# A fused five-layer block on one core: in the mixed layer the selection mask is added by TensorE, the convolution taps run on GpSimd, and search rounds and projection tiles are spread anew

## The reference

```python
def short_conv_mixer(a_in, gate_c, gate_b, conv_w):      # 256 channels, 3 taps, causal
    h = gate_c * a_in
    y = depthwise_conv3(h, conv_w)
    return gate_b * y

def dsa_mixer(q, k, v, iq, ik, iw, bias_tab):            # 4 heads of 64
    sc = relu(einsum("bqhd,bsd->bqhs", iq, ik))          # 8 index heads
    score = einsum("bqh,bqhs->bqs", iw, sc) * idx_scale
    score = where(s <= t, score, -inf)
    _, sel = top_k(score, 128)                           # 128 keys per query
    logits = q . k[sel] * 64**-0.5 + bias                # softmax over the selected keys
    ...

def moba_mixer(q, k, v, bias_tab):                       # 4 heads, all causal keys at 512 tokens
    ...

mix = concat([short_conv, pool_mixer, dsa, moba]) @ w_out
```

## Time and profile before

| | |
|---|---|
| three runs | 1729.51, 1732.86, 1734.89 us; median 1732.86 |
| the profiled execution | 1735.27 us, its span 1733.5 us, mean granted TensorE clock 0.991 |
| TensorE busy | 1659.6 us, 96% of the span |
| VectorE, ScalarE, GpSimd busy | 799.1, 768.3, 595.4 us |
| the mixed layer up to its output product | about 1067 to 1262 us from the start of the span |

### The profile page before, as it was taken

One profiled execution on the slowest core, in us unless ns is written; L12 is line 12 of the kernel. 1 busy time (PEld: TensorE's weight loads), 2 busy tenths in 40 slices (PEclk: granted clock), 3 DMA queues, 4 the chain that ended last, 5 costly groups with the idle time before them and its releaser, 6 DMA issues.

```text
span 1733.5 us, 24228 instructions
## 1 busy us (share of the span) xinstructions
PE 1659.6 (96%) x9321; PEld 1349.5 (78%) x9321; DVE 799.1 (46%) x2055; ACT 768.3 (44%) x1565; POOL 595.4 (34%) x286
## 2 busy tenths in 40 slices
PE   7899999999999999999899999998899999999998
PEld 6676779777788787778676778777678888887877
DVE  2777727456353434326677626798433111000052
ACT  4466644456343535433466624425744222212242
POOL 4322233222333323234222133372225444443423
PEclk9999999999999999999999999999999999999999
DMA  6321244232552222144222144522143333333312
GB/s 166 68 43 46 74 144 130 63 77 67 139 164 75 69 67 67 56 146 115 62 44 70 51 153 137 132 73 69 54 134 110 98 97 98 98 97 97 122 61 85
DMA packets 216046, 161.17 MB, mean 93 GB/s; under 512 B 53755, under 2 KB 197147, under 8 KB 215932
## 3 DMA queue, kind: packets, MB, share of 16 engines
q1 hardware_dynamic: 205904, 130.21, 27.0%
q10 hardware_dynamic: 9804, 29.38, 5.4%
q0 software_dynamic: 224, 0.03, 0.1%
HBM read 148.32 MB, written 11.14 MB: 92 GB/s over the span
## 4 chain that ended last, share of the span: by engine, by line
PE 65%; DVE 10%; ACT 5%; issue 2%; POOL 0%; ACTq 0%; DVEq 0%
PE banks L474 18%; PE banks L476 18%; PE banks L475 18%; PE banks L717 3%; PE banks L686 3%; PE banks L732 3%; DVE misc L2548 1%; ACT AB L1434 1%; ACT G L1558 1%; DVE misc L2535 1%; DVE top L2547 1%; DVE AB L2130 1%; ACT w_hi L1304 1%; ACT AB L1460 1%; DVE QKl L1978 1%
## 5 line engine op out<-in xcount | busy, mean ns | idle before, releaser
L2710 POOL TENSOR_TENSOR w_lo<-w_raw,w_hi 128x1024 fp32r<-128x1024 f32 (+3 forms) x253 | 572.8, 2272 | 1110.7 <-ACT w_hi L1304 1102.6
L474 PE MATMUL banks<-XTh,w_hi 128*128 128x512 f32 (+4 forms) x1216 | 452.2, 372 | 14.6 <-DVE w_lo L2431 4.0
L475 PE MATMUL banks<-XTl,w_hi 128*128 128x512 f32 (+4 forms) x1216 | 446.6, 367 | 0.0
L476 PE MATMUL banks<-XTh,w_lo 128*128 128x512 f32 (+4 forms) x1216 | 446.5, 367 | 0.0
L1304 ACT ACTIVATE w_hi<-w_raw 128x1024 fp32r<-128x1024 f32 (+3 forms) x254 | 251.0, 996 | 154.4 <-PE banks L476 110.6
L474 PEld LDWEIGHTS banks<-XTh,w_hi 128*128 128x128 f32 (+1 forms) x1216 | 230.0, 189 | 60.7 <-issue 18.7
L476 PEld LDWEIGHTS banks<-XTh,w_lo 128*128 128x128 f32 (+1 forms) x1216 | 229.9, 189 | 38.1
L475 PEld LDWEIGHTS banks<-XTl,w_hi 128*128 128x128 f32 (+1 forms) x1216 | 230.2, 189 | 36.3
L474 PE MATMUL banks<-w_hi,OTh 128*128 128x512 f32 (+1 forms) x448 | 171.9, 384 | 0.6 <-DVE QKl L1978 0.5
L476 PE MATMUL banks<-w_hi,OTl 128*128 128x512 f32 (+1 forms) x448 | 167.9, 375 | 0.0
L475 PE MATMUL banks<-w_lo,OTh 128*128 128x512 f32 (+1 forms) x448 | 167.7, 374 | 0.0
(11 more groups left out here) (204 smaller groups left out, 2336.6 us busy)
## 6 DMA issues: line engine op xcount, KB each, us to landing
w_raw<-in_w_gate_up_dram SPq DMA_DIRECT2D x44, 512.0 KB, 3.8
w_raw<-in_fox_w_in_dram SPq DMA_DIRECT2D x30, 512.0 KB, 4.1
w_raw<-in_mla_w_in_dram SPq DMA_DIRECT2D x26, 512.0 KB, 4.5
w_raw<-in_w_in_dram SPq DMA_DIRECT2D x24, 512.0 KB, 3.9
w_raw<-in_w_down_dram SPq DMA_DIRECT2D x22, 512.0 KB, 3.5
w_raw<-in_swa_w_in_dram SPq DMA_DIRECT2D x20, 512.0 KB, 3.8
w_raw<-in_mla_w_out_dram SPq DMA_DIRECT2D x16, 512.0 KB, 3.8
x_spill<-AB ACTq DMA_DIRECT2D x16, 512.0 KB, 2.8
```

The lines of the kernel that those rows point to most:

```text
L474: nc.tensor.matmul(o, ah, bh, start=first, stop=False, skip_group_check=True)
L475: nc.tensor.matmul(o, ah, bl, start=False, stop=False, skip_group_check=True)
L476: return nc.tensor.matmul(o, al, bh, start=False, stop=last, skip_group_check=True)
L2710: pool.tensor_tensor(view(w_lo, u, RING), view(w_raw, u, RAW), view(w_hi, u, RING).bitcast(F32), ALU.subtract).then_inc(lo_done, 1)
```

## The change

The change has five parts, all in the mixed layer.

1. **Index block 0 earlier.** TensorE runs `idx_block(0)` before the fourth `iq` tile, which needs only the first two; the fourth tile and the head weights use banks 6 and 7 in place of 2 and 3. ScalarE does the four Relu before it issues five small loads, VectorE the index sums before it evicts the fourth tile.
2. **Convolution taps on GpSimd.** GpSimd gets two new pieces between its `w_lo` instructions: `conv_taps` (per half one multiplication, then twice a multiplication into CONV_A and an addition) and `conv_low` (OTl of the half). VectorE loses its five instructions per half and waits for `conv_s` before it multiplies with CONV_Y.
3. **Search rounds.** In the convolution phase they go from 2, 1, 2, 2, 1 to 3, 3, 3, 3, 3; in the pooling phase they stay 3, 3, 4, 12; the other 11 (18 before) stand in `fill` as 3, 2, 3, 2, 1. As soon as a query tile's rounds are done, its mask is written to SEL_R (three instructions for one).
4. **Mask by TensorE.** For pairs 2 and 3 and t = 1, 2, 3, a product of the identity (rounded once at the start, `ident_r`) with SEL_R[t] adds the mask to the scores in the bank. VectorE's L2126 and L2127 give way to the one L2130 that all other pairs have.
5. **Tiles of the attention phase.** Each q tile goes from `fill(i, 1)` to `fill(i, 0)`, ahead of the turns and scores; the first half of the second values goes from `fill(1, 1)` to `fill(1, 0)`.

```diff
-            place[c.g], place[c.g + 1] = 2, 3
             o = begin()
...
-            tile("iq", n0=P)
...
             for n in range(6):
                 idx_block(n)
+                if n == 0:
+                    tile("iq", n0=P)
                 tile("conv")
...
             def fill(i, pos):                                  # TensorE
-                if pos == 1:
+                if pos == 0:
                     if i < 1:
                         pair_tile("q", i + 3)
+                    elif i == 1:
+                        parts.extend([unit("v"), unit("v")])
+                        value_half(parts, 0)
+                elif pos == 1:
+                    if i < 1:
                         pair_tile("k", i + 3)
                     elif i == 1:
-                        pair_values(2)
+                        value_half(parts, 1)
...
+                    if pr.sel:                                 # TensorE, scores
+                        pe.wait_ge(ident_round, 1)
+                        pe.wait_ge(sel_done, max(pr.s_chunks[ch]))
...
+                        if pr.sel and t:
+                            for x in range(2):
+                                mm = nc.tensor.matmul(bank[2 * (c.sch % 2) + x][:, cols], ident_r[:, :], SEL_R[t],
+                                                      start=False, stop=True, skip_group_check=True)
...
-                            if pr.sel and t:                   # VectorE, maxima
-                                link(nc.vector.tensor_tensor(pr.score(b, x, t), o, pr.bias(t, x), ALU.add))
-                                ins = nc.vector.tensor_tensor_reduce(pr.score(b, x, t), pr.score(b, x, t), SEL[t], 1.0, -3e38,
-                                                                     ALU.add, ALU.max, mx[:, b, 4 * x + t:4 * x + t + 1])
-                                continue
...
             for cc in range(2):                                # VectorE, convolution phase
-                idx_block(3 * cc)
+                if cc:
+                    idx_block(3)
+                    top(3)
                 c.g += 1
-                if cc:
-                    top(2)
                 idx_block(3 * cc + 1)
-                top(2)
+                top(3)
                 o = group()
                 groups_stored(dve, c.g - 1)
                 stored(nc.vector.tensor_tensor(CONV_H[:, 2:514], o[:, :], CONV_A, ALU.mult))
-                groups_stored(dve, c.g)
-                link(nc.vector.tensor_scalar(CONV_Y, CONV_H[:, 0:512], conv_w[:, cc, 0:1], None, ALU.mult))
-                for tap in (1, 2):
-                    link(nc.vector.scalar_tensor_tensor(CONV_Y, CONV_H[:, tap:tap + 512], conv_w[:, cc, tap:tap + 1], CONV_Y,
-                                                        ALU.mult, ALU.add))
                 idx_block(3 * cc + 2)
-                top(1)
+                top(3)
                 o = group()
-                groups_stored(dve, c.g - 1)
+                dve.wait_ge(conv_s, 4 * cc + 4)
+                if cc:
+                    dve.wait_ge(conv_lo, cc)
                 stored(nc.vector.tensor_tensor(otmp[:, :], o[:, :], CONV_Y, ALU.mult))
-                lo(OTl[:, cc, :], otmp[:, :], OTh[:, cc, :])
...
+            def conv_taps(cc):                                 # GpSimd
+
+                groups_stored(pool, mark["conv", cc])
+                pool.tensor_scalar(CONV_Y, CONV_H[:, 0:512], conv_w[:, cc, 0:1], None, ALU.mult)
+                for tap in (1, 2):
+                    pool.tensor_scalar(CONV_A, CONV_H[:, tap:tap + 512], conv_w[:, cc, tap:tap + 1], None, ALU.mult).then_inc(conv_s, 1)
+                    pool.wait_ge(conv_s, 4 * cc + 2 * tap - 1)
+                    pool.tensor_tensor(CONV_Y, CONV_Y, CONV_A, ALU.add).then_inc(conv_s, 1)
+                    pool.wait_ge(conv_s, 4 * cc + 2 * tap)
...
+                if u in (conv0 + 4, conv0 + 7):                # conv0: the first conv unit
+                    conv_taps((u - conv0 - 4) // 3)
+                elif u in (conv0 + 6, conv0 + 9):
+                    conv_low((u - conv0 - 6) // 3)
                 if u == pool0 + 3:
                     window_sums(0)
```

More of the change, by code:

```diff
@@ L581, in pair_values, with value_half @@
                 ready_pv[c.pair + p] = c.g
+            def value_half(parts, half):
+                o = begin()
+                for t in (2 * half, 2 * half + 1):
+                    ts = slice(t * P, (t + 1) * P)
+                    for k in range(KD):
+                        h, l = parts[k // 4]
+                        mm = three(o[:, 256 * (t % 2):256 * (t % 2) + 256], XTh[:, k, ts], XTl[:, k, ts],
+                                   h[:, k % 4, :], l[:, k % 4, :], k == 0, k == KD - 1)
+                end(mm)
             def values(head=0):
@@ L586, in values @@
                 for half in range(2):
[L587 to L594 removed]
+                    value_half(parts, half)
                 released()
@@ L1866, in _, with idx_block @@
             stored(nc.scalar.activation(iw_t[:, :, :], group()[:, 0:3 * IDX_HEADS].rearrange("p (t h) -> p t h", t=3), ACT.Copy))
+            def idx_block(n):
+                keys = CAUSAL_KEYS[1 + n // 2]
+                for h in range(4):
+                    m = 4 * n + h
+                    if h % 2 == 0:
+                        act.wait_ge(idx_s, m // 2 + 1)
+                    if n:
+                        act.wait_ge(idx_f, m - 3)
+                    nc.scalar.activation(RELU[h][:, 0:keys], bank[h][:, 0:keys], ACT.Relu).then_inc(idx_r, 1)
+            idx_block(0)
             act.dma_start(V2, consts["counts"]).then_inc(pool_in, 16)
@@ L2703, in window_sums, with conv_low @@
                 pool.wait_ge(pool_d, cc + 1)
+            conv0 = next(u for u, x in enumerate(units) if x[0] == "conv")
+            def conv_taps(cc):
[6 more added lines that the diff above has]
+                    pool.wait_ge(conv_s, 4 * cc + 2 * tap)
+            def conv_low(cc):
+                pool.wait_ge(g_hi, mark["conv_hi", cc])
+                pool.tensor_tensor(OTl[:, cc, :], otmp[:, :], OTh[:, cc, :].bitcast(F32), ALU.subtract).then_inc(conv_lo, 1)
             pool.wait_ge(pool_cst, 2)
+            pool.wait_ge(cst, N_CST)
             pool.wait_ge(lo_done, 1)
```

101 lines of the change are left out of this document (61 added, 40 removed).

## The result

The changed kernel takes 1741.41 us (median of 7 runs, 1736.68 to 1742.44), the kernel before in the same comparison 1733.29 (7 runs): ratio 1.0046, 95% interval 1.0032 to 1.0060. It is slower, by half a percent, and outside the range forecast. The profiled executions' spans are 1739.8 and 1733.5 us, 6.3 apart.

The account below looks back on a forecast made before the run. TensorE's chain, 65% of the span, was taken as the bound, with 14.8 us idle in the mixed layer and the clock to win. Terms 1.6 - 5.1 + 2.1 = -1.4 us gave a median of 1731.5 us, range 1724.5 to 1737.5.

Parts of the forecast that it names:

- Part 1: At index block 0, TensorE's 1.4 us wait for the fourth tile goes; TensorE is 1.3 us ahead.
- T: End of the second product with CONV_Y, set by VectorE's list; forecast to move +0.7 us, between -2.4 and +3.0.
- 3.2 in the second: VectorE's saving in the second conv half from losing the taps: 3.2 us, 1.54 of it for the two L2564.
- Second phase: From T through the window sums: `pooled(0)` 1.9 us later, with 1.2 for `conv_low(1)`, and `pooled(1)` 1.6 us late.
- Third phase: From `pooled(1)` to the end of `mix(0)`: 51.3 us against 56.4 before, a gain of 5.1 us.
- i = 1 and 2: From the end of `mix(0)` to the next turned tiles: 21.9 us against 19.8, 2.1 us lost, ScalarE the bound.
- three signs of a wrong forecast: T over 3 us off; TensorE waiting for `sel_done`; ScalarE's evictions at i = 1 not what `turn` waits for.
- GpSimd becomes the bound: GpSimd's list delays `pooled(0)`, perhaps with half clock, or VectorE is late for the mask: 1740 us; chance 0.10.
- Taking turns does not happen: VectorE and GpSimd do not delay each other; T at -2.4, total -4.5, 1728.4 us; within the forecast's own 0.70 case.
- All waits go: TensorE's mixed-layer idle time and low clock go: -15 us at most, a good half -8, 1725 us; chance 0.20.

Follow-up runs that it names:

- e12: Kernel before with only index block 0 moved ahead of the fourth index query tile; 1734.8 us, ratio 1.0001.
- e13: Changed kernel with search rounds placed as in the kernel before, 8 ahead of T, taps still on GpSimd; 1742.0 us, ratio 1.0048.
- e4: Changed kernel with convolution taps and low parts back on VectorE and 8 search rounds ahead of T; 1739.7 us, ratio 1.0029.
- e10: Changed kernel with GpSimd multiplying by tap 0 only, taps 1 and 2 left out (convolution result differs); 1738.5 us, ratio 1.0025.
- e3: Changed kernel with CONV_H made ahead of the rounds in the second conv half and two rounds fewer there; 1737.7 us, ratio 1.0023.
- e7: Kernel before with only the mask added by TensorE, VectorE making each width's mask behind its last round; 1741.3 us, ratio 1.0040.
- e8: Kernel before with only the query tiles of pairs 1 to 3 moved ahead of the scores; 1733.8 us, ratio 1.0000.
- e5: Changed kernel with VectorE's reciprocals of pair 1 put behind the first maxima of pair 2; 1736.5 us, ratio 1.0012.
- e9: Kernel e6 with the mask added by VectorE ahead of the maxima again, not by TensorE; 1729.1 us, ratio 0.9967.
- e2: Changed kernel, values still split, with ScalarE's weight-unit rounding moved from between pair 2's exponentials to behind the second value half; 1737.0 us, ratio 1.0014.
- e6: Changed kernel with pair 2's value halves together, CONV_H earlier with two rounds fewer, and pair 1's reciprocals behind pair 2's first maxima; 1729.4 us, ratio 0.9973.
- e14: Kernel e4 with pair 2's value halves together and pair 1's reciprocals behind pair 2's first maxima; 1734.6 us, ratio 1.0000.

## Why the prediction was wrong

The forecast was -1.4 us; A to mix(3) it is +6.4. By its own steps:

**Part 1** held: TensorE 1.4 us ahead (e12), forecast 1.3.

**T: forecast +0.7, measured +1.9.** This step failed in kind; that T lay inside its bounds all the same was luck. I let VectorE's list, stretched by turns, set T. In fact 1.4 us less (e12), 0.6 more for the taps on GpSimd (e13 against e4, 53.80 for 53.19) and 2.7 more for seven rounds (e13 against the changed kernel) make +1.9. Rows had been misread. The two L2564 of 3.75 us were counted as saved, but 2.2 of them were a stall by GpSimd's `w_lo`. So were 1.2 of the "3.2 in the second" half, where the one-input L2562 took 1.66 us for 0.49 in the first; VectorE and GpSimd in the kernel before:

```profile
1125.78 1.66 DVE L2562 TENSOR_SCALAR AB<-AB,conv_w 128x512 f32<-128x512 f32 x1
```

```profile
1124.76 2.40 POOL L2710 TENSOR_TENSOR w_lo<-w_raw,w_hi 128x1024 fp32r<-128x1024 f32 x1 [4.51 <-ACT w_hi L1304]
```

With the taps gone such a stall falls on the next index instruction (e10). And the wait for CONV_Y, 3.6 us, had no term: I compared lengths of lists and did not follow the chain from CONV_H through five instructions of GpSimd. The multiplication, 1.6 to 1.8 us for 0.8, lengthened that chain; turns-taking was the smaller thing, 1.0 us on the index instructions for my 3.1.

**Second phase: forecast +1.6 at p1, measured +4.5.** `conv_low(1)` ahead of the sums is right: T to the first pool product is 11.8 us before and 13.1 in e3, +1.3 for 1.2. On top of T's 1.9 and this 1.3 came 0.8 of half clock (T to that product 13.9 us) and 0.6 of a longer wait for the key tile's low part. That last one is in e7 too (0.8 us for 0.3), where taps and rounds stand as before, and in neither e8 nor e12: it goes with the masks that VectorE now writes width by width. TensorE's wait at the query tile was 3.8 us, as forecast, and the clock was at half behind it. PE in the changed kernel in windows (us, busy, PEclk, DMA share, GB/s):

```profile
1136.70:1142.00 5.30, 5.29 (x13) 0.50 0.41 105
...
1142.50:1148.00 5.50, 5.50 (x26) 1.00 0.25 75
```

I had kept such a stretch for a rival, with 10% of the chance.

**Third phase: forecast -5.1, measured -3.9.** The tiles, scores and the 2.8 us wait are as forecast; mix(0) took 3.82 us at half clock where 2.37 had been taken. The wait itself was a loss that the order of VectorE's list made (e5), not one that the work required. That L2127 leaves VectorE helped nothing at i = 0 either, once the reciprocals stand behind (e9).

**i = 1 and 2: forecast +2.1, measured +5.8.** This is the step that makes the forecast wrong, by 3.7 us. The exponentials of pair 2 came 11.8 us behind mix(0), for the forecast's 11.6 (whose terms, 5.1 + 5.65 + 0.6, make 11.35), and that late start cost what was said (1.9, e2). The rounding between the heads stood in the sum with its 0.95 us and no wait. That it wants the ring place of the first value unit, free only behind the second half, was not followed; ScalarE waited 2.99 us, and with the low clock behind it 4.0 were lost. An instruction that stays in its place can find its condition met later because others were moved past it.

Sum of the misses: 2.9 + 1.2 + 3.7 = 7.8, and -1.4 + 7.8 = 6.4. None of the three signs of a wrong forecast came (T was 1.2 us off, TensorE never waited for `sel_done`, ScalarE's evictions were what `turn` waited for), so they did not cover the step that failed.

Of the rivals none was it as described. "GpSimd becomes the bound" had the half clock and the late T right, but neither the multiplication's length nor `sel_done` decided. It priced the half clock behind T at 1.5 to 3.4 us, where it cost 0.8, wanted a wait "of over 4 us" for it where 3.8 was followed by one, and knew nothing of the loss behind mix(0); that its 1740 lies near the measured time is luck. "Taking turns does not happen" is refuted, and so is "All waits go". What stays open: the medians differ by 8.1 us and the profiled spans by 6.3; no run here assigns the 1.8 us between. e10, 3 us faster by the median and level in the profile, has the same gap the other way. Both lie within the spread of single executions, which is 5.8 us in the changed kernel and goes with the granted clock: 1736.7 us at 0.992, 1742.4 at 0.987.

The rule of the Trainium skill that elementwise work belongs on VectorE (GPSIMD Engine Reference, "Engine selection") is borne out for the price: a tap's multiplication took 1.6 to 1.8 us there, and 0.49 on VectorE where no `w_lo` stretched it. That section's "1-input is roughly line-rate" is not: the 0.5 us estimated from that page was a third of what was measured. For the outcome the rule did not hold: the taps on GpSimd gain 5 us in e6 against e14, where VectorE's mask was late.

## What to carry to other kernels

Follow a moved step from its input to whoever waits for its output: an engine relieved of 7.4 us of instructions can be handed 7.5 us of waiting. A stall that another engine's instruction causes goes with that instruction: take away the one that it falls on, and it falls on the next of its kind. When a sum moves to another engine, ask at what place in that engine's order its operand is now wanted; and when a group of products is split, ask which buffers stay taken in between, and who has queued for them.

## What the runs showed of the hardware

A `TENSOR_SCALAR` of 128x512 on GpSimd took 1.56 us at the least and 1.6 to 1.8 in the mean of its groups (1.97 at the most, beside VectorE's index instructions), with a constant as with a column, and so more than its `TENSOR_TENSOR` of the same shape (1.08; 1.33 here): one input less was not cheaper. In the changed kernel an index instruction of VectorE took 0.24 us more beside a tap, and 1.9 to 2.2 us more where a `w_lo` began beside it. After a wait of 2.77 us (changed kernel) and one of 2.26 us (e12) mix(0) ran at half clock, 3.82 and 4.07 us; after 2.81 us in the earlier trace rows it ran at full clock, 2.37 us. A wait's length alone does not decide it. The Trainium skill says that the chip's look at TensorE's activity is not tied to the program, so that the same program can meet it elsewhere ("TensorE: Matmul & The Clock Gate", Part 1); these rows fit that. So do the profiles of before and e8, whose instructions up to A are the same: in the 20 us ahead of A TensorE was busy for 17.05 us in both, at a granted clock of 0.91 in the one and 1.00 in the other. A gain of 1 to 2 us can so be given back where the half clock meets other products, as in e12.
